# Heads of a DeltaNet mixer: another order of v's convolution, silus, input copies and square sums

## The reference

```
qkv = silu(short_conv(h @ w_in[:, :3072], conv_w))      # 5 taps, centred, per channel
q = l2norm(q) * HEAD_K ** -0.5 ;  k = l2norm(k)
A = strict_lower((k * beta) @ k^T * decay);  u, w = (I + A)^-1 applied to v * beta and k * beta * exp(G)
for each chunk:  v_new = u - w @ S;  o = q_dec @ S + qk @ v_new;  S = S * gl + k_dec^T @ v_new
o = (o_forward + flip(o_backward)) normed * norm_g * silu(z);   y = o @ w_out
```

## Time and profile before

| | us |
|---|---|
| median of three runs (2130.76 to 2136.45) | 2133.71 |
| the profiled execution | 2131.07 |
| its span in the profile | 2129.2 |
| PE busy in the span | 1925.5 |
| VectorE busy | 1125.8 |
| ScalarE busy | 751.8 |
| POOL busy | 408.3 |

### The profile page before, as it was taken

One profiled execution on the slowest core, in us unless ns is written; L12 is line 12 of the kernel. 1 busy time (PEld: TensorE's weight loads), 2 busy tenths in 40 slices (PEclk: granted clock), 3 DMA queues, 4 the chain that ended last, 5 costly groups with the idle time before them and its releaser, 6 DMA issues. The chain is left out here.

```text
span 2129.2 us, 39348 instructions
## 1 busy us (share of the span) xinstructions
PE 1925.5 (90%) x14555; PEld 1558.5 (73%) x14556; DVE 1125.8 (53%) x1761; ACT 751.8 (35%) x1287; POOL 408.3 (19%) x316
## 2 busy tenths in 40 slices
PE   6899899899898999999999989899998998899990
PEld 4888788787885568887788766677776776677770
DVE  3566676676675554323222357655447457554438
ACT  3432332432331022221222102654446446443332
POOL 0244244244233122112121144000000000000003
PEclk7899999999999999999999998999999999999995
DMA  8133233233234443243223514975569658655354
GB/s 289 55 120 98 79 115 104 75 113 114 65 113 146 155 138 109 82 128 114 99 89 102 175 40 158 324 239 182 179 194 318 202 187 310 226 165 166 104 179 163
DMA packets 186860, 320.06 MB, mean 150 GB/s; under 512 B 26137, under 2 KB 77729, under 8 KB 186619
## 3 DMA queue, kind: packets, MB, share of 16 engines
q1 hardware_dynamic: 170683, 286.00, 40.5%
q10 hardware_dynamic: 12192, 17.00, 2.3%
q0 software_dynamic: 3744, 13.63, 1.8%
HBM read 283.89 MB, written 32.67 MB: 149 GB/s over the span
## 5 line engine op out<-in xcount | busy, mean ns | idle before, releaser
L1262 PE MATMUL pp<-whi,xTh 128*128 128x512 f32 (+1 forms) x1152 | 444.4, 386 | 21.2 <-issue 11.1
L1953 ACT ACTIVATE whi<-wring 128x1024 fp32r<-128x1024 f32 (+1 forms) x324 | 314.8, 979 | 415.9 <-PE pp L1264 361.7
L1264 PE MATMUL pp<-wlo,xTh 128*128 128x512 f32 (+1 forms) x1152 | 431.7, 375 | 0.0
L1263 PE MATMUL pp<-whi,xTl 128*128 128x512 f32 (+1 forms) x1152 | 431.4, 374 | 0.0
L2618 DVE TENSOR_TENSOR wlo<-wring,whi 128x1024 fp32r<-128x1024 f32 (+1 forms) x180 | 209.5, 1164 | 272.1 <-ACT whi L1953 222.6
L1262 PEld LDWEIGHTS pp<-whi,xTh 128*128 128x128 f32 x1152 | 218.4, 190 | 71.1 <-issue 26.1
L1264 PEld LDWEIGHTS pp<-wlo,xTh 128*128 128x128 f32 x1152 | 218.4, 190 | 39.1
L1263 PEld LDWEIGHTS pp<-whi,xTl 128*128 128x128 f32 x1152 | 218.8, 190 | 34.5
L1262 PE MATMUL pp<-whi,hTh 128*128 128x512 f32 x528 | 212.8, 403 | 9.8 <-issue 3.4
L1264 PE MATMUL pp<-wlo,hTh 128*128 128x512 f32 x528 | 206.8, 392 | 0.0
L1263 PE MATMUL pp<-whi,hTl 128*128 128x512 f32 x528 | 206.4, 391 | 0.0
(11 more groups left out here) (322 smaller groups left out, 3087.1 us busy)
## 6 DMA issues: line engine op xcount, KB each, us to landing
wring<-in_moe_w_gu SPq DMA_DIRECT2D x320, 256.0 KB, 3.7
wring<-in_ada_w SPq DMA_DIRECT2D x80, 512.0 KB, 4.8
wring<-in_moe_w_down SPq DMA_DIRECT2D x160, 256.0 KB, 3.5
wring<-in_ffn_w_gu SPq DMA_DIRECT2D x80, 256.0 KB, 3.0
wring<-in_dn_w_in SPq DMA_DIRECT2D x128, 128.0 KB, 2.7
wring<-in_ffn_w_down SPq DMA_DIRECT2D x40, 256.0 KB, 2.9
expert_in<-zeros SPq DMA_DIRECT2D x36, 256.0 KB, 3.3
wring<-in_ada_w SPq DMA_DIRECT2D x32, 256.0 KB, 5.0
```

What stands on the lines that cost most here:

```text
L1262: pe.matmul(out, hi[:, c0 + c, tt], wh, start=(first and c == 0), stop=False)
L1263: pe.matmul(out, lo[:, c0 + c, tt], wh, start=False, stop=False)
L1264: mm = pe.matmul(out, hi[:, c0 + c, tt], wl, start=False, stop=(last and c == nk - 1))
L1953: act.activation(whi[:, hs, 0:nk, 0:w], wring[:, ring_v.slot(k), 2 * s:2 * s + nk, 0:w], ACT.Copy)\
```

## The change

No instruction is added or taken away; one wait is added on PE. On ScalarE `vt_copy` 12 and 13 go ahead of `conv_input` of v; silu of q moves from behind `new_values(2)` to behind `new_values(0)`, and `chunk_high(4(h+2))` from the end of the inversion to behind it; silu of v moves from behind `new_values(3)` to behind the first `grams`; `z_silu` side 0 moves ahead of `new_values(3)`; `q_squares` and `v_tokens` move ahead of `new_values(4)`, in the opposite order. On VectorE the fourth tap of q moves ahead of update 12; the five taps of v move up, so that the first is issued in the inversion and the last behind `right_sides(2)`; and the second `a_blocks` moves ahead of `right_sides(4)`. On PE `q_square_sums` waits for `v_ready` as well, since the copy of v's transposes no longer stands ahead of q's squares on ScalarE.

```diff
--- before.py
+++ after.py
@@ -830,6 +830,7 @@
             def q_square_sums(h):
 
                 pe.wait_ge(S["sq_done"], 2 * h + 2)
+                pe.wait_ge(S["v_ready"], h + 1)
                 for t in range(T):
                     mm = pe.matmul(PP[2][:, 500 + t:501 + t], sq[:, tok(t):tok(t) + P], cm[:, ONES, 0:1], start=True, stop=True)
                 mm.then_inc(S["ss_ps"], 1)
@@ -1841,11 +1842,10 @@
                 if nx:
                     chunk_high(CHUNKS * (h + 1) + 3)
                     conv_silu(h + 1, 0)
-                    conv_input(h + 1, 2)
                 vt_copy(h, 12)
                 vt_copy(h, 13)
-                if h + 2 < H:
-                    chunk_high(CHUNKS * (h + 2))
+                if nx:
+                    conv_input(h + 1, 2)
                 for g in range(1, 6):
                     if out_head(g) == h:
                         store_mod(g)
@@ -1872,6 +1872,10 @@
                 if nx:
                     k_squares(h + 1)
                 new_values(0)
+                if nx:
+                    conv_silu(h + 1, 1)
+                if h + 2 < H:
+                    chunk_high(CHUNKS * (h + 2))
                 for d in range(2):
                     act.wait_ge(S["s_add_ps"], h * 10 + (d + 1))
                     act.wait_ge(S["state_out"], h * 32 + 1)
@@ -1888,17 +1892,16 @@
                 new_values(2)
                 if nx:
                     grams(h + 1, 0)
-                    conv_silu(h + 1, 1)
+                    conv_silu(h + 1, 2)
+                    z_silu(h + 1, 0)
                 new_values(3)
                 if nx:
-                    z_silu(h + 1, 0)
                     grams(h + 1, 1)
-                    conv_silu(h + 1, 2)
+                    q_squares(h + 1)
+                    v_tokens(h + 1)
                 new_values(4)
                 if nx:
-                    v_tokens(h + 1)
                     z_silu(h + 1, 1)
-                    q_squares(h + 1)
                 if h + 2 < H:
                     chunk_high(CHUNKS * (h + 2) + 1)
                 out_square(h)
@@ -2399,11 +2402,12 @@
                 update(h, 11)
                 if nx:
                     chunk_low(CHUNKS * (h + 1) + 3)
-                    conv(h + 1, 1, 0, 3)
+                    conv(h + 1, 1, 0, 4)
                 update(h, 12)
                 update(h, 13)
                 if nx:
-                    conv(h + 1, 1, 3, 5)
+                    conv(h + 1, 1, 4, 5)
+                    conv(h + 1, 2, 0, 1)
 
             def scan(h):
 
@@ -2470,32 +2474,29 @@
                 if nx:
                     k_sums(h + 1)
                 right_sides(1)
+                if nx:
+                    conv(h + 1, 2, 1, 2)
                 outputs(0)
                 if nx:
                     k_normal(h + 1)
-                if nx:
-                    conv(h + 1, 2, 0, 1)
+                    conv(h + 1, 2, 2, 3)
                 new_states(1)
                 outputs(1)
                 if nx:
-                    conv(h + 1, 2, 1, 2)
+                    conv(h + 1, 2, 3, 4)
                 right_sides(2)
                 if nx:
-                    conv(h + 1, 2, 2, 3)
+                    conv(h + 1, 2, 4, 5)
                 new_states(2)
                 outputs(2)
-                if nx:
-                    conv(h + 1, 2, 3, 4)
                 right_sides(3)
                 if nx:
                     a_blocks(h + 1, 0)
                 new_states(3)
                 outputs(3)
                 if nx:
-                    conv(h + 1, 2, 4, 5)
+                    a_blocks(h + 1, 1)
                 right_sides(4)
-                if nx:
-                    a_blocks(h + 1, 1)
                 outputs(4)
                 assert done[0] == 18
```

## The result

The changed kernel takes 2084.32 us (2079.61 to 2087.43) against 2132.24 us; the ratio is 0.9771, 95% interval 0.9746 to 0.9795. (The kernel before had a median of 2133.71 us when the forecast was made, and 2132.24 with one more run; 1.5 us of the distance to 2091 come from that.) The profiled execution took 2083.96 us with a span of 2082.1, 47.1 us less than before.

A forecast was written before the change was run, and what follows sets the result against it. PE and VectorE were taken to wait for order, not work, in the DeltaNet heads. 5.45 us a head over seven heads (38.1) plus 4.6 for clock gave 42.7 us: median 2091 us, range 2086 to 2108.

The forecast's parts named there:

- (c): PE's stop ahead of the second Gram in each head, 0.18 us, forecast to go.
- (d): PE's stop ahead of side 1 of z in each head, 0.69 us, forecast to go.
- (e): PE's stop of 2.60 us ahead of the v transposes, waiting for v's silu; forecast gain 2.78 us a head.
- part 4: Middle of the scan: with silu of q and of z early, stops of 0.18 and 0.69 us a head go.
- (a): PE's stop of 1.68 us ahead of the inversion's last level, waiting for ScalarE's copies; forecast to go.
- Part 6: Clock lost behind the stops comes back: 3.3 us behind (e), 1.3 us behind (a), 4.6 us in all.
- Parts 1, 2 and 3: Inversion's end to second solve: earlier copies win 1.73 us; silu(q) and chunk_high cost nothing; v's second tap costs 0.1 to 0.2.
- part 5: The v transposes follow adds(3) directly, gaining 2.78 us a head; the waits after them net +0.1 us.
- Rival 1: POOL's chunk split starts first and v's second tap waits it out in every head: 15 us, 2106 us; chance 0.17.
- Rival 2: ScalarE's state copies come behind silu(q) and chunk_high: 1.8 us a head, 2104 us; chance 0.13, including similar waits.
- Rivals 3 and 4: Hidden loads set a head's pace, no change, 2133 us; denser stream costs granted clock, 2148 us; chance 0.04 each.
- what would show it: Signs listed beforehand, among them the distance from one head's v transposes to the next dropping by about 5.5 us.

The follow-up runs named there:

- e2: The kernel before with only ScalarE's vt_copy 12 and 13 moved ahead of conv_input of v: 2126.85 us, ratio 0.9954.
- e4: The changed kernel with silu of z, side 0, behind new_values(3) again: 2095.24 us, ratio 0.9811.
- e1: The changed kernel run again, nothing changed: 2090.01 us, ratio 0.9785 to the kernel before.
- e10: The changed kernel run a third time, nothing changed: 2082.49 us, ratio 0.9771 to the kernel before.
- e5: The changed kernel with four tiny VectorE operations between right_sides(1) and v's second tap: 2100.91 us, ratio 0.9857.
- e6: The changed kernel with ScalarE's conv_input of v ahead of vt_copy 12 and 13 again: 2105.09 us, ratio 0.9878.
- e11: The kernel of e6 with v's second tap moved behind outputs(0): 2105.81 us, ratio 0.9883.
- e3: The changed kernel with v's last tap behind outputs(3) and v's silu behind q's squares again: 2112.58 us, ratio 0.9888.

## Why the prediction was right where it was, and where it failed

The chain of cause was right: the stops named went, and by the moves named. What failed is the size of some terms. In the terms of the sum, for a head at full clock, from start to start in head 2 (or head 0 for the transposes at full clock):

```
                                    forecast   measured
last level of the inversion           1.7        1.75   (e2 alone: 1.73)
second Gram (c)                       0.18       0.45
side 1 of z (d)                       0.69       0.95   (e4: 0.97)
v transposes (e)                      2.78       2.77
to the sums of q's squares            0.1        0.14
from there to the next inversion      0          0.10
sum                                   5.45       6.16
clock, all heads                      4.6        5.4
```

The step that failed is part 4: the sizes of (c) and (d) were taken from the idle time in the brackets, 0.87 us, while (a) and (e) were taken from the distance of starts. The rows of matmuls overlap: in head 2 after the change z starts at 313.33, 0.24 us ahead of the end of the solve (312.96 + 0.61), and that solve 0.16 us ahead of the end of the Gram matrices (311.84 + 1.28). A stop that takes this overlap away costs more than its bracket; and the Gram matrices took 1.38 us behind their stop, 1.28 without. By starts, (c) and (d) are 1.40 us together, 0.53 more: 3.7 us over seven heads. e4 shows it for (d). The small terms make another 1.3 us.

Part 6 was 0.8 us short: I counted half of the clock lost behind (a), and all of it came back. Its figures from the earlier trace rows, 1.35 us behind (a) and 1.67 behind (e), are a little above what the distances show, 1.16 and 1.56. Parts 1, 2 and 3 held, part 5 to 0.05 us. By these terms the sum should have read 7 x 6.16 + 5.4 = 48.5 us.

The heads gave 47.2: 45.5 from the first last level to the eighth, and 1.74 of head 0 ahead of it. The 1.3 us that are short of 48.5 lie in two places. From head 4 to 5 it is the 0.25 us of `a_blocks`. In the last distance, 63.19 us against 66.51, PE waited longer than before at three points: 1.14 us in place of 0.79 at the second solve, 0.98 in place of 0.76 for POOL at the start of the inversion, and 0.93 in place of 0.18 ahead of a `mod_burst`. For the last the profile names no releaser, and it varies: it was 0.23 and 0.30 us in e1 and e10, where this distance is 62.49 and 62.62.

What lies outside the heads moved by as much as the whole error of the sum, and cancelled. The first last level came 2.94 us later than before though head 0 had won 1.74 there, so the start lost 4.7 us; from the eighth last level to the end 1442.4 us became 1437.9, a gain of 4.5. That the two cancel, and the span shows 47.1 us, is chance. The windows of the first 60 us, before and after, show the loss at the start as granted clock:

```profile
0.00:60.00 60.00, 40.74 (x208) 29.80 (x210) 23.17 (x45) 19.21 (x39) 4.76 (x8) 0.75 0.74 257
```

```profile
0.00:60.00 60.00, 39.98 (x191) 27.12 (x192) 20.93 (x37) 16.86 (x33) 4.76 (x8) 0.67 0.74 256
```

0.75 against 0.67, in code that the change does not touch. Why the end was faster is open. My range left no room for this: its own low end of 2086 allowed 5 us below 2091, which the mis-sized terms used up.

Rival 1 did not occur in the changed kernel, but by a margin of 0.27 us in head 2 and of 0.06 in head 1 (228.81 against 228.87); e5 shows its price. Rival 2 did not either: 0.95 us of slack. Rivals 3 and 4 are out: no load stands among PE's waits in the heads (the profile names no releaser for the 0.93 us in the inversion of head 7), and the clock granted in the heads rose from 0.98 to 1.00. Of "what would show it", the distance of the v transposes from head to head fell from 78.5 us on average to 71.5, more than the 5.5 named, as clock and mis-sized terms come with it.

## What to carry to other kernels

Price a stop on TensorE by the distance between the starts of its neighbours, with and without it, and not by the idle time shown: the small ones here cost 1.4 and 2.5 times their bracket. Where an order is written by hand, look for an instruction that waits ahead of one whose inputs are long there; moving the second ahead cost nothing in most places here (the move of `a_blocks` cost 0.34 us a head, that of the tap 0.35 us once), and the 5.4 us of clock that were lost behind the stops came back with it. A VectorE operation like this tap (128x644, 0.88 us by itself) should not stand in the critical order at a moment when a GpSimd operation like the chunk split (128x1024, 2.34 us) may start: begun 0.02 us behind the split, the tap took 3.00 us (e5). There a delay of 0.4 us turned into 2.3, and in e6 a late wait on another engine brought the same meeting about.

## What was not expected of the hardware

A stop of about the same length is followed by half clock (granted 0.50) in some heads and not in others: behind 1.68 us in two of seven before, in five in e6 and four in e11; behind 2.60 us in two of seven before, in three in e2 and in five in e3. Where it came without a further stop, it cost 1.2 to 1.6 us each time.

A half clock stretch on TensorE flipped the order in which VectorE's tap and GpSimd's split start, and so made a stop longer: the tap 0.72 us behind the split in place of 0.26 ahead of it, the stop ahead of the second solve 1.79 us in place of 0.79, and the head 75.28 us in place of 73.19 with the same instructions (e6).

What lies outside the heads varies by itself: the first last level came at 145.5 to 152.2 us in the thirteen profiled executions (of which 1.7 us are the copies of head 0), and the stretch behind the eighth took 1438 to 1449 us, in code that is the same in all of them.
